# Two-layer hybrid block on one core: gate projections of the mixers spread between other matmuls, and another order of the work at each mixer's entry

## The chip, the cores and the metric

The kernel runs on one core of one Trainium2 chip, as one launch. The metric is the device time of that core in microseconds (us), lower is better. The kernel before was timed three times: 1550.9, 1551.62 and 1552.19 us, median 1551.62 us.

## The reference, cut to what matters

All tensors are float32. A sequence of 256 tokens with 1024 features goes through two layers of a first block and one layer of a second block. Every sublayer is a residual update.

```python
for l in range(2):                                   # first block
    f = swiglu(rms_norm(x, ffn1_pre_g[l]), w_gu, w_down);  x = x + 0.5 * rms_norm(f, ffn1_post_g[l])
    m = hybrid_mixer(rms_norm(x, mix_pre_g[l]), ...);      x = x + rms_norm(m, mix_post_g[l])
    f = swiglu(rms_norm(x, ffn2_pre_g[l]), w_gu, w_down);  x = x + 0.5 * rms_norm(f, ffn2_post_g[l])
# second block: one mixer of other kind (s5, short conv, sparse attention), then one swiglu

def hybrid_mixer(h, ...):
    pa, pb, pc = split(h @ w_in)                     # 768 | 1286 | 512 columns
    gate_a, rec_a = split(pa, 2)
    rec = causal_dwconv(rec_a)
    ya = rg_lru(rec, ...) * gelu(gate_a)             # r, i = sigmoid(...); a = exp(..r); u = sqrt(..tanh..)*(i*rec); scan
    yb = ssd_mixer(pb, ...)                          # conv, silu, decays exp(segsum), (CB * decays) @ (x*dt), norm
    yc = chunk_sgu(pc, ...)                          # u, v = split(gelu(uv)); layer_norm(v); u * (w @ v)
    return concatenate([ya, yb, yc]) @ w_out
```

## The kernel before

**Weights.** All weights come as one stream of chunks of 128 x 1024 float32 (512 KB each), read by the SyncE queue into a ring of six slots (`raw`). Float32 products are made from two parts: ScalarE rounds a chunk to its high part (`split_hi`, line 445, tile `whi`), VectorE or GpSimd subtracts to get the low part (`split_lo`, line 452; `split_lo_pool`, line 461; tile `wlo`), and TensorE makes three matmuls per product (lines 466 to 468: high x high, high x low, low x high). The read of chunk c+6 waits until the low part of chunk c is made; the high part of chunk c+6 waits until TensorE has used chunk c (semaphore `consumed`). Chunks are used in the order of the stream, and `consumed` and `lo_ready` count them.

**Engines.** Each engine has its own instruction list, written by hand; semaphores tie them together. Nothing reorders them. Products land in four banks, `work0` to `work3`; the list `BANKED` says in which order a mixer's results take them, so a result waits (`begin`) until the result four places ahead of it has been taken out. `BY_ACT` and `BY_DVE` say which engine takes it out, and `JOBS` numbers TensorE's finished results.

**A mixer of the first block** (function pairs `mix_pe`, `mix_act`, `mix_dve`, `mix_pool`). TensorE projects `zdt` (z and dt, chunks 0 to 3, the fourth holding only 48 columns in use), `xbc` (chunks 4 to 10), `rec` (11 to 13); then transposes (`xtok0`, `xtok1`), running sums of decays (`csb0` to `csb2`, lines 975 and 976), the recurrence's gates (`lru0` to `lru2`, line 984), `csb3` to `csb5`; then the three gate projections `gate0` to `gate2` (chunks 14 to 16, 24 matmuls of 256 columns each); the six head products `y0` to `y5` (lines 997 to 1001, matmuls of 64 columns); the projections `uv0` and `uv1` (chunks 18 to 21, 24 matmuls of 512 columns each); and the output projection in eight steps. `y3` to `y5` need `weights(1)` of VectorE (line 1196). Before the fourth of the eight output steps stand the small matmuls of `gated` (line 1014), which need the layer norm of `uv` (`vln`, line 1272). ScalarE swaps its function tables (ACT_TABLE_LOAD) between Exp, Sigmoid, Exp and Tanh, Gelu, Sqrt and Gelu. `C_GATE` is 14, `C_PAD` 17 (a chunk of zeros, two columns of which are split), `C_UV` 18.

**Entry into a mixer** (`mix_enter_act`, `mix_enter_dve`), three times: into both mixers of the first block and into the second block's mixer. While TensorE ends the projection before, VectorE updates the first half (t = 0) of x, makes its mean square (`norm_mean`), GpSimd its power (`norm_pow`, line 541, tile `xrstd`), VectorE scales it (`scaled`, line 589, tile `xn`), TensorE transposes it (`turn_xn`, line 647), ScalarE writes its high part (`high`, line 523, tile `xboth`) and VectorE the low part (`low`, line 531). Among these stand the same steps for the second half: `weighted` (line 563), `post_squares` (line 500), `post_mean` (line 545), `update` (line 569). The first matmul of `zdt0` (or of `q0` in the second block) needs the first `low`.

## Time and profile before

| | before |
|---|---|
| median of 3 runs | 1551.62 us |
| the profiled execution, its own time | 1547.13 us |
| its span, first to last instruction | 1545.2 us |
| TensorE (PE) busy | 1479.9 us, 96% |
| VectorE (DVE) busy | 1146.5 us, 74% |
| ScalarE (ACT) busy | 772.0 us, 50% |
| GpSimd (POOL) busy | 140.4 us, 9% |
| mean granted TensorE clock | 0.977 of full speed |

The profile shows one execution. Times inside it count from the start of its span. The first mixer of the first block runs from about 203 to 310 us, the second from about 692 to 801 us, and the second block's mixer begins at about 996 us. The two mixers of the first block repeat each other at a distance of 490.1 us. A wait of TensorE costs time of the kernel wherever TensorE is what sets the end. The granted clock is told as a share of 2.4 GHz: 1.00 is 2.4 GHz and 0.50 is 1.2 GHz.

### The profile page before, as it was taken

How to read it: one execution, taken by the hardware profiler on the slowest of the kernel's cores; microseconds unless marked ns; L12 is line 12 of the kernel's file. 1: busy time of each engine (PE TensorE's matmuls, PEld its weight loads, DVE VectorE, ACT ScalarE, POOL GpSimd, SP SyncE). 2: the span in 40 equal slices, each digit the busy share in tenths (PEclk: the TensorE clock that was granted, in tenths of full speed). 3: DMA queues.
4: the chain of work that ended last, by engine and by line, in shares of the span. 5: the costliest groups of instructions: out<-in, count | busy, mean ns of one | idle time of the engine just before them, and what ended most of it. 6: DMA issues, size and time to landing. Idle time of an engine off the chain costs nothing.

```text
span 1545.2 us, 24303 instructions
## 1 busy us (share of the span) xinstructions
PE 1479.9 (96%) x8495; PEld 1283.3 (83%) x8495; DVE 1146.5 (74%) x1835; ACT 772.0 (50%) x1257; POOL 140.4 (9%) x139
## 2 busy tenths in 40 slices
PE   6999999899999999999899999979998999999999
PEld 5888888788888888879778888777987789888887
DVE  4877776777777777777767777866589967577776
ACT  5344366464444544346645434464588755354432
POOL 0000024100000000005110000101332310000000
PEclk9999999999999999999899999989898999999999
DMA  7665644446655566565344655535522245646652
GB/s 289 193 201 190 192 150 151 132 151 196 201 190 191 208 199 195 188 192 153 109 158 156 204 189 190 166 123 171 192 83 80 72 132 184 190 150 201 194 188 85
DMA packets 71072, 261.74 MB, mean 169 GB/s; under 512 B 8016, under 2 KB 8016, under 8 KB 70736
## 3 DMA queue, kind: packets, MB, share of 16 engines
q1 hardware_dynamic: 69696, 253.79, 50.8%
q10 hardware_dynamic: 1296, 6.85, 1.2%
q8 instruction: 54, 0.88, 0.2%
q14 instruction: 26, 0.21, 0.0%
HBM read 259.56 MB, written 1.05 MB: 169 GB/s over the span
## 4 chain that ended last, share of the span: by engine, by line
PE 87%; DVE 7%; ACT 4%; issue 2%; DMA 1%; POOL 0%; DVEq 0%; ACTq 0%
PE work L728 24%; PE work L729 12%; PE acc L466 8%; PE acc L468 8%; PE acc L467 8%; PE work L466 8%; PE work L467 7%; PE work L468 7%; DVE wlo L452 2%; PE work L1428 1%; PE acc L1457 1%; ACT whi L445 1%; DVE frac L1837 0%; PE work L1429 0%; ACT xboth L523 0%
## 5 line engine op out<-in xcount | busy, mean ns | idle before, releaser
L452 DVE TENSOR_TENSOR wlo<-raw,whi 128x1024 fp32r<-128x1024 f32 x460 | 548.2, 1219 | 206.3 <-ACT whi L445 203.0
L728 PE MATMUL work<-xboth,whi 128*128 128x512 f32 x1600 | 560.7, 393 | 0.0
L445 ACT ACTIVATE whi<-raw 128x1024 fp32r<-128x1024 f32 x480 | 474.9, 1039 | 48.9 <-PE work L468 35.4
L729 PE MATMUL work<-xboth,wlo 128*128 128x256 f32 x1600 | 445.3, 278 | 0.0
L728 PEld LDWEIGHTS work<-xboth,whi 128*128 128x128 f32 x1600 | 299.7, 187 | 68.6
L729 PEld LDWEIGHTS work<-xboth,wlo 128*128 128x128 f32 x1600 | 301.2, 188 | 4.3
L808 ACT ACTIVATE sg<-sg 128x256 f32<-128x256 f32 x100 | 41.8, 418 | 476.1 <-DVE sg L849 476.1
L468 PE MATMUL acc<-whi,hlo 128*128 128x512 f32 x440 | 173.8, 395 | 0.0
L467 PE MATMUL acc<-wlo,hhi 128*128 128x512 f32 x440 | 173.6, 395 | 0.0
L466 PE MATMUL acc<-whi,hhi 128*128 128x512 f32 x440 | 173.5, 394 | 0.0
L466 PE MATMUL work<-xboth,whi 128*128 128x256 f32 x488 | 144.4, 296 | 8.2 <-DVE wlo L452 8.2
L467 PE MATMUL work<-xboth,whi 128*128 128x256 f32 x488 | 141.7, 290 | 0.0
L468 PE MATMUL work<-xboth,wlo 128*128 128x256 f32 x488 | 141.5, 290 | 0.0
L466 PEld LDWEIGHTS work<-xboth,whi 128*128 128x128 f32 x488 | 98.0, 201 | 9.1 <-issue 8.8
L466 PEld LDWEIGHTS acc<-whi,hhi 128*128 128x128 f32 x440 | 82.5, 187 | 19.9
L468 PEld LDWEIGHTS acc<-whi,hlo 128*128 128x128 f32 x440 | 82.5, 187 | 19.9
L467 PEld LDWEIGHTS work<-xboth,whi 128*128 128x128 f32 x488 | 97.9, 201 | 0.1
L468 PEld LDWEIGHTS work<-xboth,wlo 128*128 128x128 f32 x488 | 97.4, 200 | 0.0
L467 PEld LDWEIGHTS acc<-wlo,hhi 128*128 128x128 f32 x440 | 82.5, 187 | 15.7
L466 PE MATMUL work<-whi,xboth 128*128 128x512 f32 (+2 forms) x192 | 79.2, 413 | 13.4 <-DVE wlo L452 8.0
L847 DVE TENSOR_REDUCE sg<-work 128x256 f32<-128x512 f32 x100 | 68.7, 687 | 12.0 <-PE work L729 12.0
L467 PE MATMUL work<-wlo,xboth 128*128 128x512 f32 (+2 forms) x192 | 75.9, 395 | 0.0
(435 smaller groups left out, 2022.0 us busy)
## 6 DMA issues: line engine op xcount, KB each, us to landing
raw<-stream SPq DMA_DIRECT2D x480, 512.0 KB, 3.7
par<-pm ACTq DMA_DIRECT2D x2, 1644.5 KB, 7.3
pfa<-pf_a ACTq DMA_DIRECT2D x3, 516.0 KB, 3.6
pfb<-pf_b ACTq DMA_DIRECT2D x2, 516.0 KB, 8.0
x<-x_in SPq DMA_DIRECT2D x2, 512.0 KB, 5.8
out<-x SPq DMA_DIRECT2D x2, 512.0 KB, 2.6
par<-pm ACTq DMA_DIRECT2D x1, 820.0 KB, 4.3
pre<-pf_a ACTq DMA_DIRECT2D x1, 4.0 KB, 4.0
```

The lines of the kernel that those rows point to most:

```text
L445: nc.scalar.activation(chunk(whi, place, c)[:, cols], chunk(raw, place, c)[:, cols], ACT.Copy).then_inc(hi_ready, 1)
L452: nc.vector.tensor_tensor(chunk(wlo, place, c)[:, cols], chunk(raw, place, c)[:, cols], chunk(whi, place, c)[:, cols].bitcast(F32), ALU.su ...
L466: return [nc.tensor.matmul(o, lhi, rhi, start=start, stop=False), nc.tensor.matmul(o, lhi, rlo, start=False, stop=False), nc.tensor.matmul ...
L467: nc.tensor.matmul(o, lhi, rlo, start=False, stop=False),
L468: nc.tensor.matmul(o, llo, rhi, start=False, stop=stop)]
L728: nc.tensor.matmul(o[:, :], hi[:, k * P:(k + 1) * P], xboth[:, k, :], start=k == 0, stop=False)
L729: m = nc.tensor.matmul(o[:, 0:S], lo[:, k * P:(k + 1) * P], xhi[:, k, :], start=False, stop=k == KD - 1)
L808: nc.scalar.activation(sg[:, j % 2, :], sg[:, j % 2, :], ACT.Silu).then_inc(sg_ready, 1)
L847: nc.vector.tensor_reduce(sg[:, j % 2, :], both_halves(gate), AX.X, ALU.add).then_inc(gsum_ready, 1)
L1428: nc.tensor.matmul(bank2(f"sc{r}", slice(b * S, b * S + nkeys(t))), qT[:, h, t * P:(t + 1) * P], kT[:, 2 * b + h // 4, 0:nkeys(t)], start= ...
L1457: m = nc.tensor.matmul(acc[at:at + 32, 1, k % 2 * S:(k % 2 + 1) * S], left, rotated[:, r % 2, i // 2, i % 2, :], start=i == 0, stop=i == 3)
```

## The change

Three edits.

1. In the mixers of the first block the gate projections no longer stand together. `gate0` comes behind `rec2`, `gate1` behind `csb2`, `gate2` behind `csb5`. ScalarE takes each out with a plain copy, and applies Gelu once to all three (768 columns) behind the Sqrt; VectorE waits for that (`gate_ready`). `uv0` moves ahead of `y0` to `y5`, and its first product now counts the pad chunk as used. The bank order changes with it.
2. `tokens` waits for the low part of each weight chunk when it comes to it, not for the last of them at the start (in all three mixers).
3. At all three entries `scaled` of the first half stands straight behind its mean, and the low part of the fourth chunk (`split_lo [3]`) behind the first two `low`. ScalarE makes the first `high` steps between the two halves of `post_squares`.

```diff
-BANKED = (["zdt0", "zdt1"] + [f"xbc{b}" for b in XBC_ORDER] + ["rec0", "cs", "rec1", "rec2", "xtok0", "xtok1", "csb0", "csb1", "csb2"]
-          + [f"lru{b}" for b in range(AB)] + ["csb3", "csb4", "csb5", "gate0", "gate1", "gate2", "uv0", "uv1", "sgu0", "sgu1"]
+BANKED = (["zdt0", "zdt1"] + [f"xbc{b}" for b in XBC_ORDER] + ["rec0", "cs", "rec1", "rec2", "gate0", "xtok0", "xtok1", "csb0", "csb1", "csb2", "gate1"]
+          + [f"lru{b}" for b in range(AB)] + ["csb3", "csb4", "csb5", "gate2", "uv0", "uv1", "sgu0", "sgu1"]
...
-JOBS += [f"y{h}" for h in range(HEADS)] + ["uv0", "sgu0", "sgu1", "ybt0", "ybt1", "ybt2", "yct0", "yct1"]
+JOBS += ["uv0"] + [f"y{h}" for h in range(HEADS)] + ["sgu0", "sgu1", "ybt0", "ybt1", "ybt2", "yct0", "yct1"]
...
             squares(act, q, 0)
-            post_squares(act, p, 1, end, c)
-            high(act, q, g, range(0, 4))
+            post_squares(act, p, 1, end, c, [0])
+            high(act, q, g, range(0, 2))
+            post_squares(act, p, 1, end, c, [1])
+            high(act, q, g, range(2, 4))
             squares(act, q, 1)
...
             norm_mean(dve, q, 0)
-            split_lo(dve, place, [3])
+            scaled(dve, q, r, 0)
             weighted(dve, p, 1, gp, end)
             post_mean(dve, p, 1, eps[1])
-            scaled(dve, q, r, 0)
             low(dve, q, g, range(0, 2))
+            split_lo(dve, place, [3])
             update(dve, p, 1)
...
-                pe.wait_ge(lo_ready, place.count(c + chunks - 1))
...
                 for k in range(KD):
+                    if k == 0 or ((k + 1) * n - 1) // CH > (k * n - 1) // CH:
+                        pe.wait_ge(lo_ready, place.count(c + ((k + 1) * n - 1) // CH))
...
+                    if padded and k == 0:
+                        recent[0].then_inc(consumed, 1)
...
             channels("rec2", C_REC + 2)
+            channels("gate0", C_GATE)
...
             for h in range(3):
                 sums(h)
+            channels("gate1", C_GATE + 1)
...
-            for b in range(AB):
-                channels(f"gate{b}", C_GATE + b)
+            channels("gate2", C_GATE + 2)
+            begin(pe, BANKED, "uv0")
+            done("uv0", tokens("uv0", 0, C_UV, 2 * CW, padded=True)[-1])
             xdt_ready.wait(pe, T)
...
-                m = nc.tensor.matmul(acc[:, 0, cols], w[:, 0:P], xdt[:, 0, cols], start=True, stop=True)
-                if h == 0:
-                    m.then_inc(consumed, 1)
+                nc.tensor.matmul(acc[:, 0, cols], w[:, 0:P], xdt[:, 0, cols], start=True, stop=True)
...
-            begin(pe, BANKED, "uv0")
-            done("uv0", tokens("uv0", 0, C_UV, 2 * CW)[-1])
             begin(pe, BANKED, "uv1")
...
+            def gated(b):
+                projected(C_GATE + b)
+                emptied(f"gate{b}", nc.scalar.activation(gateT[:, b, :], bank(f"gate{b}", slice(0, S)), ACT.Copy))
+                split_hi(act, place, [C_GATE + b + 6])
+
+            gated(0)
             decays(0)
+            gated(1)
...
             decays(1)
-            for b in range(AB):
-                projected(C_GATE + b)
-                emptied(f"gate{b}", nc.scalar.activation(gateT[:, b, :], bank(f"gate{b}", slice(0, S)), ACT.Gelu_apprx_tanh))
-                split_hi(act, place, [C_GATE + b + 6])
+            gated(2)
             mult2.wait(act, 1)
             mult_ready.inc(nc.scalar.activation(th[:, :, :], th[:, :, :], ACT.Sqrt))
             split_hi(act, place, [C_PAD + 6])
+            evac.wait(act, BY_ACT.index("gate2") + 1)
+            gate_ready.inc(nc.scalar.activation(gateT[:, :, :], gateT[:, :, :], ACT.Gelu_apprx_tanh))
...
-            evac.wait(dve, BY_ACT.index("gate2") + 1)
+            gate_ready.wait(dve, 1)
             ya32.inc(nc.vector.tensor_tensor(rg[:, :, :], rg[:, :, :], gateT[:, :, :], ALU.mult))
```

How the instructions stand. First TensorE in a mixer, from the transposes on. Before, `xtok0` (line 968) is followed by the sums (lines 975 and 976) and the recurrence's gates (line 984):

```order
L968 MATMUL work1<-ident,xbcc 128x128 [waits m_rec_conv,m_xbc_act]
L968 MATMUL work1<-ident,xbcc 128x128 x2
L968 MATMUL work2<-ident,xbcc 128x128 [waits m_vec]
L968 MATMUL work2<-ident,xbcc 128x128 x2
L975 MATMUL work3<-upper,ad 128x256 [waits m_rec_conv]
L976 MATMUL work3<-upper,ad 128x128
L975 MATMUL work0<-upper,ad 128x256 [waits m_rec_conv]
L976 MATMUL work0<-upper,ad 128x128
L975 MATMUL work1<-upper,ad 128x256 [waits m_vec]
L976 MATMUL work1<-upper,ad 128x128
L984 MATMUL work2<-recc,par 128x256 [waits m_rec_conv,m_vec]
```

The same place in the changed kernel, where the lines of code are 975, 982 and 983; it begins at the last matmul of `gate0` and ends at the first three of `gate1`:

```order
L469 MATMUL work1<-xboth,wlo 128x256
L975 MATMUL work2<-ident,xbcc 128x128 [waits m_vec,m_xbc_act]
L975 MATMUL work2<-ident,xbcc 128x128 x2
L975 MATMUL work3<-ident,xbcc 128x128 [waits m_rec_conv]
L975 MATMUL work3<-ident,xbcc 128x128 x2
L982 MATMUL work0<-upper,ad 128x256 [waits m_rec_conv]
L983 MATMUL work0<-upper,ad 128x128
L982 MATMUL work1<-upper,ad 128x256 [waits m_evac]
L983 MATMUL work1<-upper,ad 128x128
L982 MATMUL work2<-upper,ad 128x256 [waits m_vec]
L983 MATMUL work2<-upper,ad 128x128
L467 MATMUL work3<-xboth,whi 128x256 [waits lo_ready,m_vec]
```

A whole gate projection now stands ahead of the transposes and another behind `csb2`; `csb1` waits for ScalarE's copy of `gate0` (`m_evac`) instead of for the convolution.

Then ScalarE in the same stretch, from the end of `rec2`'s split to the first Sigmoids. Before:

```order
L1065 ACTIVATE xbcc<-xbcc 128x256 x3
L445 ACTIVATE whi<-raw 128x1024 x2
L1069 ACT_TABLE_LOAD
L1069 ACTIVATE dm<-dm 128x1152
L1101 ACT_TABLE_LOAD
L1101 ACTIVATE rg<-work,par 128x256
```

and now:

```order
L1070 ACTIVATE xbcc<-xbcc 128x256 x3
L446 ACTIVATE whi<-raw 128x1024 x2
L1106 ACTIVATE gateT<-work 128x256
L446 ACTIVATE whi<-raw 128x1024
L1074 ACT_TABLE_LOAD
L1074 ACTIVATE dm<-dm 128x1152
L1106 ACTIVATE gateT<-work 128x256
L446 ACTIVATE whi<-raw 128x1024
L1114 ACT_TABLE_LOAD
L1114 ACTIVATE rg<-work,par 128x256
```

A copy and a chunk split stand ahead of the decays' Exp and again between it and the Sigmoids; behind the Sqrt one table load and one Gelu of 768 columns come, and the table load ahead of the Gelu of `uv0` is gone.

Last VectorE at the entry. Before:

```order
L545 SCALAR_TENSOR_TENSOR xms<-xss 128x1
L452 TENSOR_TENSOR wlo<-raw,whi 128x48
L563 TENSOR_TENSOR xn<-acc,pfa 128x512 x2
L545 SCALAR_TENSOR_TENSOR pms<-pss,peps 128x1
L589 TENSOR_SCALAR xn<-x,xrstd 128x512 x2
L531 SCALAR_TENSOR_TENSOR xboth<-work,par,xboth 128x128 x4
L569 SCALAR_TENSOR_TENSOR x<-xn,prstd,x 128x512 x2
```

and now:

```order
L546 SCALAR_TENSOR_TENSOR xms<-xss 128x1
L590 TENSOR_SCALAR xn<-x,xrstd 128x512 x2
L564 TENSOR_TENSOR xn<-acc,pfa 128x512 x2
L546 SCALAR_TENSOR_TENSOR pms<-pss,peps 128x1
L532 SCALAR_TENSOR_TENSOR xboth<-work,par,xboth 128x128 x4
L453 TENSOR_TENSOR wlo<-raw,whi 128x48
L570 SCALAR_TENSOR_TENSOR x<-xn,prstd,x 128x512 x2
```

The scaling of the first half moved up past the split, the product and the mean of the second half; the low part of the fourth chunk moved down behind the first low parts of x. In the second block's entry that chunk is a full one of 1024 columns.

## Rows read from the trace of the kernel before

**Rows 1.** Waits of TensorE: total us, times, longest us.

```profile
PE work L466 <- DVE wlo L452: 19.8, 3, 8.2
...
PE acc L997 <- DVE dm L1196: 6.5, 2, 3.2
```

**Rows 2.** Timeline of TensorE, first mixer: start, duration, instruction [idle before, releaser].

```profile
249.38 0.82 PE L968 MATMUL work<-ident,xbcc 128*128 128x128 f32 x6
...
251.73 0.70 PE L975 MATMUL work<-upper,ad 128*128 128x256 f32 x2 [0.88 <-DVE recc L1162]
...
253.58 2.86 PE L984 MATMUL work<-recc,par 128*128 128x256 f32 x12
...
258.88 0.70 PE L975 MATMUL work<-upper,ad 128*128 128x256 f32 x2 [1.79 <-ACT ig L1102]
...
260.34 0.38 PE L466 MATMUL work<-xboth,whi 128*128 128x256 f32 x1
...
269.06 0.33 PE L997 MATMUL acc<-xdt,dm 128*128 128x64 f32 x2
...
274.43 0.43 PE L997 MATMUL acc<-xdt,dm 128*128 128x64 f32 x2 [3.25 <-DVE dm L1196]
...
285.23 0.39 PE L466 MATMUL work<-whi,xboth 128*128 128x512 f32 x1
...
290.67 0.40 PE L466 MATMUL acc<-whi,yahi 128*128 128x512 f32 x1
```

**Rows 3.** Windows: PE, PEld, DVE, ACT, POOL busy (count); granted clock, DMA.

```profile
274.40:278.00 3.60, 3.57 (x19) 3.57 (x19) 3.46 (x5) 0.00 (x0) 0.00 (x0) 0.55 0.37 137
...
768.50:772.00 3.50, 3.50 (x10) 2.73 (x10) 3.27 (x7) 2.50 (x6) 1.35 (x2) 0.50 0.00 0
772.00:776.00 4.00, 4.00 (x17) 3.26 (x16) 3.11 (x4) 0.86 (x1) 2.38 (x3) 0.86 0.46 133
```

**Rows 4.** Timeline of ScalarE, first mixer.

```profile
256.69 1.28 ACT L1101 ACT_TABLE_LOAD   x1
...
259.78 0.50 ACT L1102 ACTIVATE ig<-work,par 128x256 f32<-128x256 f32 x1
...
263.67 0.50 ACT L1107 ACTIVATE th<-rg,psp 128x256 f32<-128x256 f32 x1
...
266.81 1.05 ACT L445 ACTIVATE whi<-raw 128x1024 fp32r<-128x1024 f32 x1
...
272.01 0.84 ACT L1114 ACTIVATE th<-th 128x768 f32<-128x768 f32 x1
```

**Rows 5.** Timeline of VectorE, first mixer.

```profile
271.89 1.22 DVE L452 TENSOR_TENSOR wlo<-raw,whi 128x1024 fp32r<-128x1024 f32 x1
273.02 1.35 DVE L1196 TENSOR_TENSOR dm<-dm,acc 128x1152 f32<-128x1152 f32 x1
```

**Rows 6.** Timeline of VectorE (layer norm's end) and TensorE (`gated`), first mixer.

```profile
296.96 0.42 DVE L1272 TENSOR_TENSOR vx<-vx,par 128x256 f32<-128x256 f32 x1
...
299.07 1.89 PE L1014 MATMUL work<-vx,par 128*128 128x64 f32 x16
```

**Rows 7.** Timelines of GpSimd, ScalarE and VectorE at the first mixer's entry.

```profile
202.06 0.55 POOL L541 TENSOR_TENSOR xrstd<-xms,small 128x1 f32<-128x1 f32 x1 [2.73 <-DVE xms L545]
...
203.27 0.60 ACT L500 ACTIVATE h<-acc 128x512 f32<-128x512 f32 x1 [0.74 <-DVE xn L563]
...
205.13 2.17 ACT L523 ACTIVATE xboth<-work,par 128x128 fp32r<-128x128 f32 x8 [1.18 <-PE work L647]
...
204.12 0.88 DVE L589 TENSOR_SCALAR xn<-x,xrstd 128x512 f32<-128x512 f32 x2
...
205.79 1.13 DVE L531 SCALAR_TENSOR_TENSOR xboth<-work,par,xboth 128x128 fp32r<-128x128 f32 x4 [0.79 <-ACT xboth L523]
```

**Rows 8.** Timelines of GpSimd and VectorE at the second block's entry.

```profile
995.05 1.46 POOL L541 TENSOR_TENSOR xrstd<-xms,small 128x1 f32<-128x1 f32 x1 [3.03 <-DVE xms L545]
...
999.29 1.13 DVE L531 SCALAR_TENSOR_TENSOR xboth<-work,pfa,xboth 128x128 fp32r<-128x128 f32 x4 [0.82 <-ACT xboth L523]
```

More of the change, by code:

```diff
@@ L395, in block_program @@
         ya32 = mixsig("ya32", 1)
+        gate_ready = mixsig("gate", 1)
         dexp = mixsig("dexp", 2)
@@ L490, in halves_of, with post_squares @@
             return slice(h * D // 2, (h + 1) * D // 2)
-        def post_squares(act, p, t, end, c):
-            for h in range(2):
+        def post_squares(act, p, t, end, c, parts=range(2)):
+            for h in parts:
                 if h == 0:
@@ L920, in channels, with tokens @@
                 m[-1].then_inc(consumed, 1)
-            def tokens(name, t, c, n, at=0, first=False):
+            def tokens(name, t, c, n, at=0, first=False, padded=False):
                 chunks = -(-KD * n // CH)
-                pe.wait_ge(lo_ready, place.count(c + chunks - 1))
                 hi, lo = chunk(whi, place, c, chunks), chunk(wlo, place, c, chunks)
@@ L1326, in tokens @@
                 chunks = -(-KD * n // CH)
-                pe.wait_ge(lo_ready, place.count(c + chunks - 1))
                 hi, lo = chunk(whi, place, c, chunks), chunk(wlo, place, c, chunks)
@@ L1330, in tokens @@
                 for k in range(KD):
+                    if k == 0 or ((k + 1) * n - 1) // CH > (k * n - 1) // CH:
+                        pe.wait_ge(lo_ready, place.count(c + ((k + 1) * n - 1) // CH))
                     if first:
```

## The prediction

> **What bounds the kernel now.** I read the share of busy time first: TensorE is busy 96% of the span, so the end moves only where TensorE waits, or where it runs at the lower clock. So I read TensorE's waits next. The longest group, on the low parts of weight chunks, belongs mostly to the second block [rows 1]; its 8.2 us wait there stands behind a chain of VectorE and ScalarE that the change does not touch. The wait of the head products on `weights(1)` is 6.5 us in two times, one in each mixer [rows 1]. The timeline of the first mixer then shows three waits: 0.88 us in front of a sum, 1.79 us in front of another and 3.25 us in front of `y3` [rows 2], 5.92 us together. The windows show what follows the longest one: the granted clock is 0.55 behind it in the first mixer, and 0.50 and then 0.86 in the second [rows 3]. So the wait is paid twice, once as idle time and once as slow matmuls.
>
> **The most that the mixer can give.** From the transposes (249.38) to the output projection (290.67) TensorE takes 41.29 us [rows 2]. Its work at full clock, from the same rows: the three gate projections take 269.06 - 260.34 = 8.72 us, 2.91 each. `uv1` is 24 matmuls of 512 columns from 285.23 to 290.67, 5.44 us, so both uv take 10.88. `y0` to `y2` take 274.43 - 3.25 - 269.06 = 2.12 us, six 4.24. Transposes, six sums and the three `lru` take 260.34 - 249.38 - 0.88 - 1.79 = 8.29 us. The sum is 32.13, which is 9.16 less than 41.29: 5.92 of waits and 3.24 of lower clock (y3 to uv1 took 16.24 us against 13.00 at full clock).
>
> **The new waits in the mixer.** I follow the new order from 249.38.
> `gate0` ends at 252.3. Transposes and three sums: two sums together take 260.34 - 258.88 = 1.46 at most, so these four pieces take about 2.6, and `gate1` starts at about 254.9 and ends at 257.8. ScalarE can take `gate0` out at 252.4 (a copy of 256 columns is priced by the nearest activation, 0.50 or less [rows 4]), which is before the second sum wants the bank, and has split the next chunk (1.05 us) by 253.9, long before the decays' Exp, which waits on VectorE. So the copy and split of `gate0` cost nothing; the cover is ScalarE's idle time in front of that Exp.
> Behind `gate1` it differs. ScalarE copies at 257.9, splits until 259.3, and only then loads the table for the Sigmoids. Before, that load began at 256.69 [rows 4]. So Sigmoid, Exp and Tanh come about 2.6 us later: the last Sigmoid ends at 262.9 instead of 260.28, the last Tanh at 266.8 instead of 264.17 [rows 4]. TensorE meanwhile does `lru` (254.9 + 2.9 = 257.8, to about 260.5; before it took 2.7) and `csb3` to 261.2, then waits for the Sigmoids' banks, some 0.3 us in front of `csb4` and less than 0.1 in front of `csb5` and `gate2`. Together 0.5. `gate2` runs from 262.9 to 265.8.
> `uv0` then wants four chunks one after another. The low parts of the first three are there (VectorE has idle time for them). The fourth stands on VectorE behind three products that need the last Tanh: those ended at 271.89, that is 2.85 us of work, so now 266.8 + 2.9 = 269.7, and with the split of 1.22 [rows 5] the chunk is ready at 270.9. TensorE reaches it after 18 of its 24 matmuls, at 265.8 + 4.1 = 269.9. It waits 1.0 us. This is the one use of edit 2 that matters here: with the old wait TensorE would have stood 5.1 us in front of `uv0`. `y0` starts at 272.3. `weights(1)`, 1.35 us behind that split [rows 5], ends at 272.2, and `y3` wants it at 274.4: the 3.25 us wait is gone with 2 us to spare.
> New waits make 1.5 us. Against that, two sums that started 251.73 and 253.58 took 1.85 us [rows 2], 0.4 more than the pair at 258.88; they waited for banks that VectorE emptied late, and now the `gate0` in front gives it time. So I take 9.16 - 1.5 + 0.4 = 8.1, and for what else of that kind the 8.29 may hold I add 0.4: **8.5 us in the first mixer** (bounds: 6 if each new wait is doubled and that credit is nil; 9.2 if none arises).
> The second mixer's slow stretch is longer. 0.50 instead of 0.55 over about 7.5 us, and 0.86 over 4 us where the first mixer was at full clock [rows 3], is 0.4 + 0.5 us more work at the low rate. **9.3 us in the second mixer.**
>
> **Gelu, Copy and tables.** The Gelu moves behind the Sqrt: a table load of 1.28 and a Gelu of 768 columns, priced as the Sqrt of 768 columns, 0.84 [rows 4]. From mult2 at 269.7: Sqrt, a split, the load and the Gelu end at about 274.5. VectorE's `weights(1)`, product and scans run until 275.1, so the Gelu is hidden by 0.6 us. If it were not, `ya32` and the low part of ya would be late, which the output projection wants only at 281.9; VectorE has that about 2 us earlier. Cost nil.
> The load row is 1.28 us, so it ends at 257.97; the last of the six Sigmoids starts at 259.78, which leaves five activations of 0.36 us each between and no room for more [rows 4]. The Trainium skill, page ScalarE: Activation LUTs, section What ACT_TABLE_LOAD costs, gives about 1283 ns for the load and adds about 1380 ns of drain at each switch. The trace agrees on the load and shows no such drain. By the page, two switches (Sigmoid, Exp) in front of the last Tanh would make it 2.8 us later than in my chain, the wait in `uv0` 3.8 us, and the whole gain some 13.3 instead of 18.9; with the row against it this case is worth 0.01.
>
> **The entries.** In the first mixer GpSimd ends the power at 202.61. Scaling can begin at 202.65; its first half takes 0.44. From the scaled half to the first `high` it took 205.13 - 204.56 = 0.57. So ScalarE begins at 203.66 instead of 205.13, 1.5 us earlier. But now the four activations of the first two steps (0.27 each) come ahead of the second half's square, which took 0.72 to VectorE's mean, and the mean (0.13) stands ahead of the first `low`: 203.66 + 1.09 + 0.72 + 0.13 = 205.6 against 205.79 [rows 7]. So the first matmul comes 0.2 us earlier, not 1.5. The later update of the second half starts where it did: the early mean costs 0.9 on one side and the split of 48 columns is small. Same in the second mixer. In the second block's entry GpSimd took 1.46 us beside a full VectorE split; that split is gone from beside it, so I take 0.55 (bounds 0.55 and 1.46). Then low parts begin at 995.60 + 2.98 = 998.6 instead of 999.29 [rows 8]: 0.7 us (bounds -0.2 and 0.7). The full split of 1.22 us now lies in front of the update of the second half, which is then 0.5 us late, but the matmuls that need it come 3 us after the first. The gain reaches the end, since in ScalarE's list the load of the second block's parameters, and the chain behind it, follow a `high` that waits for TensorE. Entries: 0.2 + 0.2 + 0.7 = **1.1 us**. The later low part also delays the SyncE queue's read six chunks on by about 4.6 us; that chunk is used more than 15 us later, so nothing.
>
> **The sum.** 8.5 + 9.3 + 1.1 = 18.9 us. Against the profiled execution: 1547.1 - 18.9 = 1528.2. That execution lay 4.5 us below the median of the runs, and I carry the difference over: 1551.6 - 18.9 = **1532.7 us**.
>
> **The rivals.**
> A. *As above*, 0.59: 1529 to 1536.
> B. *The clock falls anyway*, 0.15. The y block is 4.2 us of matmuls of 64 columns between a short wait and `uv1`. For it: the windows' 0.55 came right behind matmuls of this kind. Against it: with 0.88 and 1.79 us waits and small matmuls from 249 to 260 the next gate projection still ran at full rate, 2.9 us. It would leave 3.24 us per mixer unpaid: 18.9 - 6.5 = 12.4, 1539.2 us. The Trainium skill, page TensorE: Matmul & The Clock Gate, Part 1, says that the rate follows how busy TensorE has been recently, which would speak for this rival if small matmuls count little.
> C. *The time is given back behind uv*, 0.12. `gated` ran at 299.07, and the layer norm ended at 297.38, 1.7 us before [rows 6]. Now VectorE comes to the layer norm with its list full: it must first make the y sums (behind y5, at about 276.5), ya's low part, two splits and the norm of yb, by my count until about 283, while `uv1` ends at about 281.9. Before, it stood idle there. I count 0.6 to 1.3 us of delay, just inside 1.7. If it takes 3 to 4 us instead, each mixer loses 2 us: 1537 us.
> D. *Slower*, 0.04. One wait decides it: `uv0` stands before its fourth chunk until the Tanh chain is through. It becomes a loss over 0.2% when this wait is 12 us or more a mixer instead of 1.0, i.e. the low part comes after about 281 instead of 270.9; then 2 x 11 - 18.9 = +3.1, 1554.7 us and more. Only a ring of waits among the new bank order could do that; I find none.
> E. *No change*, 0.03: weights' reads become the bound, as TensorE now asks for the chunks of `uv` and the output 9 us sooner; DMA share 0.37 to 0.46 in the windows speaks against [rows 3]. 1551 us.
> F. *A switch of tables costs twice the row*, 0.01: each late step behind two switches, 13.3 us in all, 1538.3 us.
> G. *More*, 0.06: the earlier transposes also keep the clock up at the entries, and no new wait in the mixers: 24 us, 1527.5 us.
>
> **Numbers.** Predicted 1532.7 us. The range goes from G to B, with 2 us beyond B in case part of C comes with it: 1527 to 1541 us. Two executions of this kernel that differ by under 0.2% (3.1 us) can't be told apart. Faster by more than that: A, B, C, F and G, 0.93; within it 0.03; slower 0.04.
>
> **What would show it.** In the changed kernel's trace: no wait of the y products on `weights(1)`; one wait of about 1 us inside `uv0` on a low part and about 0.3 us before the fifth sum; granted clock 1.00 from the transposes to the output projection; that stretch together with `gate0` about 32.6 us long; 45 instead of 47 table loads; at the entries the transposes 1.5 us earlier but the first `zdt0` matmul only 0.2. The prediction is wrong if the clock falls in the y block, if `gated` waits for the layer norm, or if the Sigmoids come more than 3 us later than they did.

## The result and the profile after

The changed kernel takes **1529.71 us** (median of 4 runs, 1526.19 to 1532.01), the kernel before 1551.26 us beside it (4 runs, 1549.57 to 1552.19): the ratio is 0.986 with a 95% interval of 0.9839 to 0.9881. That is 21.55 us less, where 18.9 were forecast; the time forecast was 1532.7 us, between 1527 and 1541. On a second chip the same pair gave 1530.85 against 1549.33 us, ratio 0.9881 (0.9866 to 0.9896), or 18.5 us. The profiled execution after is the longest of its four, 1532.01 us (span 1530.1 us), and lies 15.1 us below the profiled one of before. So the two traces show 6.4 us less than the medians do. Where 5 us of gain go in the profiled pair is told below.

The page of the changed kernel, TensorE and its clock in 40 slices:

```profile
span 1530.1 us, 24313 instructions
...
PE 1474.6 (96%) x8495; PEld 1278.1 (84%) x8495; DVE 1146.3 (75%) x1835; ACT 770.7 (50%) x1257; POOL 140.3 (9%) x139
...
PEclk9999999999999999999999999979998999999999
```

TensorE's waits in the changed kernel (total us, times, longest):

```profile
PE work L467 <- DVE wlo L453: 21.5, 5, 8.2
PE work L467 <- DVE xboth L532: 9.6, 9, 2.0
...
PE work L650 <- DVE xn L590: 2.3, 3, 1.0
PE acc L467 <- DVE xboth L1294: 1.7, 2, 0.9
PE work L982 <- ACT ig L1115: 0.7, 2, 0.3
```

The wait of the head products on `weights(1)`, 6.5 us in two times [rows 1], has no row any more. The waits on low parts went from 3 to 5 times and by 1.7 us: the two new ones are those inside `uv0`. The 1.79 us in front of the fifth sum [rows 2] became 0.33.

TensorE in the first mixer, changed kernel:

```profile
251.39 0.82 PE L975 MATMUL work<-ident,xbcc 128*128 128x128 f32 x6
...
260.63 0.70 PE L982 MATMUL work<-upper,ad 128*128 128x256 f32 x2 [0.33 <-ACT ig L1115]
...
270.15 0.50 PE L467 MATMUL work<-whi,xboth 128*128 128x512 f32 x1 [0.83 <-DVE wlo L453]
...
271.64 0.33 PE L1006 MATMUL acc<-xdt,dm 128*128 128x64 f32 x2
...
281.38 0.39 PE L468 MATMUL acc<-wlo,yahi 128*128 128x512 f32 x1
...
289.55 1.89 PE L1019 MATMUL work<-vx,par 128*128 128x64 f32 x16
```

`gate0` starts at 248.51 and the output projection at 281.15, 32.64 us where the same work took 41.29 [rows 2]. Only waits of 0.33 and 0.83 us are left in it. The windows of the same stretch (PE, PEld, DVE, ACT, POOL busy, granted clock, DMA share, GB/s):

```profile
262.00:266.00 4.00, 4.00 (x32) 3.83 (x31) 2.19 (x5) 3.91 (x9) 0.00 (x0) 1.00 0.63 216
266.00:270.15 4.15, 3.32 (x15) 2.43 (x13) 4.06 (x5) 4.12 (x5) 0.00 (x0) 1.00 0.25 99
270.15:274.20 4.05, 4.05 (x30) 3.79 (x30) 3.95 (x5) 3.27 (x4) 0.00 (x0) 1.00 0.42 130
274.20:278.20 4.00, 4.00 (x26) 3.53 (x25) 3.48 (x7) 1.62 (x4) 0.44 (x2) 1.00 0.01 5
```

The clock is 1.00 (2.4 GHz) in every one, where 0.55 stood before behind the 3.25 us wait [rows 3]. ScalarE and VectorE behind it:

```profile
265.42 0.49 ACT L1120 ACTIVATE th<-rg,psp 128x256 f32<-128x256 f32 x1
...
271.31 1.28 ACT L1127 ACT_TABLE_LOAD   x1
272.61 0.84 ACT L1127 ACTIVATE gateT<-gateT 128x768 f32<-128x768 f32 x1
```

```profile
268.88 1.22 DVE L453 TENSOR_TENSOR wlo<-raw,whi 128x1024 fp32r<-128x1024 f32 x1
270.01 1.35 DVE L1208 TENSOR_TENSOR dm<-dm,acc 128x1152 f32<-128x1152 f32 x1
...
274.44 0.96 DVE L1262 TENSOR_TENSOR rg<-rg,gateT 128x768 f32<-128x768 f32 x1
...
288.19 0.43 DVE L1284 TENSOR_TENSOR vx<-vx,par 128x256 f32<-128x256 f32 x1
```

The Gelu ends at 273.45, 1.0 us before VectorE asks for it. The fourth low part ends at 270.10, where `uv0` resumes. The layer norm ends at 288.62, 0.9 us before `gated` at 289.55; this slack was 1.7 us [rows 6]. The changed kernel has 45 table loads where the kernel before has 47.

TensorE at the first mixer's entry, the turn of the first half and the first product of `zdt0`, first before and then after:

```profile
204.66 1.09 PE L647 MATMUL work<-ident,xn 128*128 128x128 f32 x8 [2.15 <-DVE xn L589]
206.55 0.67 PE L466 MATMUL work<-whi,xboth 128*128 128x390 f32 x1 [0.80 <-DVE xboth L531]
```

```profile
202.67 1.09 PE L650 MATMUL work<-ident,xn 128*128 128x128 f32 x8 [0.68 <-DVE xn L590]
205.78 0.67 PE L467 MATMUL work<-whi,xboth 128*128 128x390 f32 x1 [2.02 <-DVE xboth L532]
```

The turn comes 1.5 us sooner behind the matmul ahead of it (0.68 us of wait for 2.15), and most of that is waited for again in front of the first product.

**Where the gain stands in the two traces.** Starts of the same instructions of TensorE, before and after:

| place | before | after | gained so far |
|---|---|---|---|
| turned second half, mixer 1 | 212.43 | 211.55 | 0.88 |
| behind mixer 1 | 315.87 | 306.49 | 9.38 |
| first `zdt0` matmul, mixer 2 | 695.53 | 685.83 | 9.70 |
| turned second half, mixer 2 | 702.57 | 691.74 | 10.83 |
| behind mixer 2 | 806.83 | 786.63 | 20.20 |
| second block, behind its 8.2 us wait | 1027.91 | 1007.75 | 20.16 |
| end of span | 1545.2 | 1530.1 | 15.1 |

Nearly all that the change touches is through at 20.2 us. The second block's later part has the same code in both, but for the wait per chunk in `kv0` and `kv1`, and the same long waits; it took 5 us longer. The whole of it, first before and then after:

```profile
1027.91:1545.20 517.29, 498.72 (x3203) 438.67 (x3203) 383.67 (x609) 276.05 (x467) 62.19 (x45) 0.97 0.46 149
```

```profile
1007.75:1530.10 522.35, 503.70 (x3203) 442.90 (x3203) 383.75 (x609) 276.07 (x467) 62.13 (x45) 0.95 0.46 147
```

TensorE is idle for 18.6 us in both (517.29 - 498.72 and 522.35 - 503.70). The same 3203 matmuls are what took 5.0 us longer, at a lower mean clock.

The changed kernel's other three runs had mean clocks of 0.982 to 0.984 and spans of 1524.3 to 1528.0 us, the profiled one 0.980. A second trace of the changed kernel, from another chip, has 520.1 us for the part that took 522.35 here, and the other kernels of this study, which do not change that part any further, lie between 517.4 and 521.9. So the profiled pair understates the gain by what the clock did in a part whose work and waits are the same in both. There is one trace of the kernel before; its execution was 4.1 us below the median of its runs, so a part of the difference lies in which executions were profiled. Whether this part runs a little slower behind the change on average is not shown.

**The mixers in all traces.** From the turned second half to the first matmul behind the mixer, us:

| kernel | mixer 1 | mixer 2 |
|---|---|---|
| before | 103.44 | 104.26 |
| changed | 94.94 | 94.89 |
| changed, second trace | 94.96 | 95.00 |
| mixer alone | 94.95 | 94.99 |
| entries alone | 103.45 | 103.56 |
| `uv0` waits for all four chunks | 101.23 | 101.42 |
| head products ahead of `uv0` | 101.49 | 102.46 |
| Gelu at each copy | 96.21 | 96.20 |
| fourth low part early | 93.81 | 93.79 |
| low parts of x ahead of the mean | 95.00 | 94.97 |
| all three, two traces | 93.03, 93.02 | 93.05, 93.00 |
| filled wait | 94.98 | 95.01 |

Where no long wait stands in it, a mixer takes the same time to about 0.1 us in all traces of the same mixer code. These rows therefore say more about each edit in the mixers than the medians can.

### The profile page after: what moved, and what is told of

Its sections match the earlier page's. It is cut to its first block, busy times and chain, and to the rows that moved or that the text cites. A ratio compares the mean times of both kernels' runs of the same rounds, so it can differ in the third digit from the quotient of the medians.

```text
span 1530.1 us, 24313 instructions
## 1 busy us (share of the span) xinstructions
PE 1474.6 (96%) x8495; PEld 1278.1 (84%) x8495; DVE 1146.3 (75%) x1835; ACT 770.7 (50%) x1257; POOL 140.3 (9%) x139
## 4 chain that ended last, share of the span: by engine, by line
PE 86%; DVE 7%; ACT 4%; issue 2%; POOL 1%; DMA 1%; DVEq 0%; ACTq 0%
PE work L731 24%; PE work L732 12%; PE work L467 8%; PE acc L469 7%; PE acc L467 7%; PE work L469 7%; PE acc L468 7%; PE work L468 7%; DVE wlo L453 2%; PE work L1441 1%; ACT whi L446 1%; PE acc L1470 1%; DVE x L570 0%; ACT xboth L524 0%; PE work L1442 0%
## 5 line engine op out<-in xcount | busy, mean ns | idle before, releaser
L538 POOL TENSOR_TENSOR prstd<-pms,small 128x1 f32<-128x1 f32 x12 | 6.6, 548 | 750.9 <-DVE pms L546 750.9
```

The lines of the kernel that those rows point to most:

```text
L538: nc.gpsimd.tensor_tensor(prstd[:, t:t + 1], pms[:, t:t + 1], small[:, 0:1], ALU.pow).then_inc(prstd_ready, 1)
```

## The experiments

The first four ran on one chip, beside 14 runs of the kernel before with a median of 1549.72 us.

**The mixer alone.** The new order and the waits per chunk stay; the entries are as before.

```diff
-            post_squares(act, p, 1, end, c, [0])
-            high(act, q, g, range(0, 2))
-            post_squares(act, p, 1, end, c, [1])
-            high(act, q, g, range(2, 4))
+            post_squares(act, p, 1, end, c)
+            high(act, q, g, range(0, 4))
...
-            scaled(dve, q, r, 0)
+            split_lo(dve, place, [3])
             weighted(dve, p, 1, gp, end)
             post_mean(dve, p, 1, eps[1])
+            scaled(dve, q, r, 0)
             low(dve, q, g, range(0, 2))
-            split_lo(dve, place, [3])
```

> The changed kernel with the order of the entries as before (edits 1 and 2 alone). Theory (the gain lies in the waits of the mixers and the low clock behind them): about 18 us faster than before, with the stretch from the end of rec2 to the output projection 32.6 us long in both mixers against 41.3 before; the first matmul of zdt0 as late after the last matmul of the down projection as before (about 4.4 us). Rival (the entries carry a good part through the clock): under 16 us faster.

Measured: 1532.99 us (1531.51 to 1533.98), ratio 0.9894 (0.9878 to 0.9911), 16.7 us less than before. The waits inside the mixers are 0.33 and 0.83 us as in the changed kernel. By the milestones its mixers gained 8.49 and 9.27 us, as in the changed kernel, and the first `zdt0` matmul stands 4.04 us behind the last matmul ahead, as before (about 4.4 were expected). The mixers carry most of the gain.

**The entries alone.** The kernel before, with the changed entries and the waits per chunk in `tokens`; the gate projections, `uv0`, the Gelu and the table loads as before.

> The kernel before with the entries of the change and the wait for each chunk in turn (edits 2 and 3 alone). Theory: 0.2 us earlier at each of the first two entries and 0.7 at the third, 1 to 2 us in all and within the spread of runs; the transposes start 1.4 us earlier but TensorE waits 2.0 us behind them. Rival (earlier transposes keep the clock up): 4 us or more faster, with the granted clock of the entry's 8 us clearly above 0.8. In the mixers the wait for each chunk alone should change nothing, since y3's wait stands.

Measured: 1546.25 us (10 runs, 1542.57 to 1552.46), ratio 0.9987 (0.9971 to 1.0002), 3.5 us less by the medians, while the interval reaches no change. The two halves add up to 16.7 + 3.5 = 20.2 us, between the 21.55 and 18.5 of the whole on other chips; since the 3.5 may be nothing, the sum shows only that nothing large is missing. The ten runs fall into two groups of five: 1542.57 to 1545.08 us at mean clocks of 0.979 and 0.980, and 1547.42 to 1552.46 at 0.972 to 0.978. None of the 14 runs of before is under 1548.45. The trace is of the first group, and its products behind the waits of 2.02 us at the second and third entry ran at full clock, at the first they did not:

```profile
205.90:211.56 5.66, 5.66 (x24) 5.63 (x25) 4.82 (x12) 1.50 (x5) 1.81 (x2) 0.75 0.25 93
694.45:699.58 5.13, 4.79 (x25) 4.14 (x25) 4.47 (x12) 1.50 (x5) 1.80 (x2) 1.00 0.31 102
995.59:1001.91 6.32, 5.81 (x24) 4.46 (x25) 4.90 (x12) 1.50 (x5) 2.31 (x13) 1.00 0.29 83
```

So the rival (the new entries keep the clock up) is not excluded: it fits this execution, and not the changed kernel's, whose clocks at the same three places were 0.73, 0.71 and 0.76. Its waits show the mixers untouched and the wait of the entries at 2.0:

```profile
PE work L466 <- DVE xboth L531: 10.1, 10, 2.0
PE acc L1000 <- DVE dm L1199: 6.5, 2, 3.2
```

**`uv0` waits for all four chunks.** The changed kernel, with the old form of the wait for `uv0` alone:

```diff
+                if padded:
+                    pe.wait_ge(lo_ready, place.count(c + chunks - 1))
```

> The changed kernel, but uv0 waits at its start for the low part of all four chunks. Theory 1 (a wait is paid once): TensorE stands 5.1 us before uv0 in place of 0.8 inside it, so 3.9 us a mixer, some 8 us slower than the changed kernel. Theory 2 (a wait of this length also drops the clock, as the 3.25 us wait did): the granted clock behind it near 0.5 for some microseconds, about 3 us more a mixer, some 14 us slower than the changed kernel.

Measured: 1542.27 us (1541.78 to 1543.83), ratio 0.9957 (0.994 to 0.9974). Against the ratios of the changed kernel on two chips, 0.9860 and 0.9881, this gives back 12 to 15 us. Its timeline and windows of the first mixer:

```profile
271.86 0.77 PE L467 MATMUL work<-whi,xboth 128*128 128x512 f32 x1 [4.96 <-issue]
```

```profile
266.90:271.80 4.90, 0.00 (x0) 0.00 (x0) 4.05 (x5) 4.87 (x7) 0.00 (x0) 0.79 0.29 107
271.80:275.80 4.00, 3.94 (x9) 3.15 (x10) 3.90 (x5) 3.25 (x4) 0.00 (x0) 0.50 0.44 135
275.80:279.80 4.00, 4.00 (x19) 3.27 (x17) 1.22 (x2) 0.98 (x2) 0.00 (x0) 0.90 0.01 2
279.80:283.60 3.80, 3.80 (x37) 3.80 (x36) 0.00 (x0) 0.00 (x0) 0.00 (x0) 1.00 0.00 0
```

The wait is 4.96 us instead of 0.83 (5.1 were forecast for it), and behind it the clock is 0.50 (1.2 GHz) for 4 us and 0.90 for 4 more: 4 x 0.50 + 4 x 0.10 = 2.4 us. A mixer loses 4.13 + 2.4 = 6.5 us, two lose 13.1; by the milestones they lost 6.3 and 6.5. Idle time and slow matmuls behind it are both needed for the measured loss; idle time alone makes 8.3. The second reason for this kernel's time, that a wait is paid twice, is thereby shown by an edit that adds one.

**The head products ahead of `uv0`.** The changed kernel, with the gates spread, but `y0` to `y5` before `uv0` again:

```diff
-            begin(pe, BANKED, "uv0")
-            done("uv0", tokens("uv0", 0, C_UV, 2 * CW, padded=True)[-1])
             xdt_ready.wait(pe, T)
...
+            begin(pe, BANKED, "uv0")
+            done("uv0", tokens("uv0", 0, C_UV, 2 * CW)[-1])
             begin(pe, BANKED, "uv1")
```

> The changed kernel with y0 to y5 ahead of uv0, gates spread all the same. Theory: y3 waits 4.2 us for weights(1), longer than the 3.25 before, since the gates no longer cover it; by the wait alone 3.2 us a mixer slower than the changed kernel, with the clock's fall 6.5; in all 6.5 to 13 us slower than it. Rival (spreading the gates carries the gain, the place of uv0 is worth little): under 4 us slower than the changed kernel.

Measured: 1543.77 us (1542.56 to 1544.28), ratio 0.9959 (0.9945 to 0.9973), again 12 to 15 us given back. Its timeline and windows:

```profile
272.81 0.69 PE L1004 MATMUL acc<-xdt,dm 128*128 128x64 f32 x2 [4.24 <-DVE dm L1210]
```

```profile
272.90:276.90 4.00, 4.00 (x19) 4.00 (x20) 3.75 (x5) 2.00 (x3) 0.00 (x0) 0.50 0.35 130
276.90:280.90 4.00, 4.00 (x13) 3.13 (x13) 3.88 (x6) 2.00 (x5) 2.00 (x3) 0.62 0.00 0
280.90:284.90 4.00, 4.00 (x19) 3.29 (x18) 2.75 (x5) 0.60 (x1) 1.73 (x2) 1.00 0.59 176
```

The wait on `weights(1)` is back and longer than before, 4.24 instead of 3.25 us, because the gates that filled this time now stand further ahead. Per mixer: 4.24 - 0.83 of waits and 4 x 0.50 + 4 x 0.38 = 3.5 of clock, 6.9 us, 13.9 in two; by the milestones the two lost 6.6 and 7.6. So without the move of `uv0` about 6 of the 20 us are kept, and that with the new entries, which this kernel has too: its mixers are 1.95 and 1.80 us shorter than before, so spreading the gates alone is worth about 3.8 of the 17.9 us that the mixers gained. The two moves are one edit: the gates fill the early waits, and `uv0` takes the place that they left.

The next four ran on another chip, beside 9 runs of the kernel before with a median of 1551.14 us.

**Gelu at each gate's copy.** The changed kernel, with a Gelu of 256 columns in place of each copy and none behind the Sqrt. This adds a table load in front of the Sigmoids' chain.

```diff
-                emptied(f"gate{b}", nc.scalar.activation(gateT[:, b, :], bank(f"gate{b}", slice(0, S)), ACT.Copy))
+                emptied(f"gate{b}", nc.scalar.activation(gateT[:, b, :], bank(f"gate{b}", slice(0, S)), ACT.Gelu_apprx_tanh))
```

> The changed kernel with a Gelu of 256 columns in place of each copy and none behind the Sqrt. ScalarE's list gets more table loads; one of them stands between gate1 and the Sigmoids. By the load's row (1.28 us) the last Tanh, the low part that uv0 waits for and the fifth sum's bank come 1.3 us later: 1.3 us a mixer, 2.6 in all. By 2.66 us for each switch: 2.7 us a mixer or more, over 5 in all. A rival: the second load, ahead of the Sqrt, makes VectorE late too and costs the output projection time.

Measured: 1534.69 us (1529.29 to 1535.58), ratio 0.9884 (0.9866 to 0.9902). Its waits on the Sigmoids and the first of them:

```profile
PE work L981 <- ACT ig L1114: 3.1, 2, 1.6
```

```profile
262.83 0.70 PE L981 MATMUL work<-upper,ad 128*128 128x256 f32 x2 [1.57 <-ACT ig L1114]
...
272.36 0.50 PE L466 MATMUL work<-whi,xboth 128*128 128x512 f32 x1 [0.81 <-DVE wlo L452]
```

The wait before the fifth sum grew from 0.33 to 1.57, by 1.24 us a mixer: the chain is later by one load of 1.28 us and by nothing more. Both mixers took 1.3 us longer. The rival that the load ahead of the Sqrt costs time too is out, since it would come on top of that. In the time the 2.5 us of two mixers can't be told from the changed kernel (ratios 0.9860 and 0.9881); the trace is what settles this.

**The fourth low part ahead of the three products.** The changed kernel with `split_lo(dve, place, [C_UV + 3])` moved up behind that of `C_UV + 2`.

> The changed kernel with the low part of uv0's fourth chunk on VectorE ahead of the three products that wait for the Tanh, not behind them. Theory: the 0.83 us wait inside uv0 goes, weights(1) comes at most as late as now and y3 has slack: 0.8 us a mixer, 1.7 in all. Rival (VectorE's chain to the output projection is as late as TensorE): the wait comes back in front of y3 or of the output projection and nothing is gained.

Measured: 1528.73 us (1525.91 to 1530.53), ratio 0.9856 (0.9841 to 0.9871). Both 0.83 us waits are gone, and nothing came in their place. Each mixer is 1.1 us shorter, more than the 0.8 expected: in the changed kernel the matmul behind this wait starts 1.21 us behind the one ahead and the next one 0.34 us later, where such matmuls else follow each other at 0.23 us, which makes 0.98 + 0.11 = 1.1. The median does not resolve it. The waits on low parts:

```profile
PE work L467 <- DVE wlo L453: 19.7, 3, 8.1
```

**Low parts of x ahead of the mean of p.** At the entries `low(dve, q, g, range(0, 2))` stands before `post_mean(dve, p, 1, eps[1])`.

> The changed kernel with the first two low parts of x on VectorE ahead of the second half's mean at all three entries. Theory (the first matmul waits for the mean that stands ahead of the low part, not for the transposes): first matmul of zdt0 0.9 us earlier, TensorE's wait there 1.1 instead of 2.0 us; 1 to 3 us in all. Rival: the update of the second half comes later and q0 or zdt0 waits at its fifth product.

Measured: 1529.45 us (1528.43 to 1530.15), ratio 0.9861 (0.9846 to 0.9876). The timeline of the first mixer's entry:

```profile
206.39 0.41 PE L467 MATMUL work<-whi,xboth 128*128 128x390 f32 x1 [1.11 <-DVE xboth L532]
...
209.54 0.44 PE L467 MATMUL work<-whi,xboth 128*128 128x390 f32 x1 [0.78 <-DVE xboth L532]
```

The first wait fell from 2.02 to 1.11 us, and a second of 0.78 arose in front of the fifth product: the next x parts are not ready earlier. Most of the 0.9 us goes to this new wait. Of the 1 to 3 us expected the median shows none (ratios 0.9860 and 0.9881 for the changed kernel).

**All three.** The fourth low part early, the low parts before the mean, and the split of the chunk behind `gate1` (`C_GATE + 7`) moved on ScalarE behind the last Sigmoid.

```diff
-                split_hi(act, place, [C_GATE + b + 6])
+                if b != 1:
+                    split_hi(act, place, [C_GATE + b + 6])
...
+            split_hi(act, place, [C_GATE + 7])
```

> The changed kernel with both last steps together, and the high part of one chunk (gate1's place in the ring) moved behind the Sigmoids, so that they start 1.05 us earlier. Theory: the 0.33 us wait in front of the fifth sum goes as well; 1.3 us a mixer from the mixers and 0.9 at each entry, about 5 us faster than the changed kernel. Rival: the clock's dips of one execution and another make more difference than that.

Measured: 1525.65 us (1525.07 to 1526.37), ratio 0.9836 (0.9822 to 0.9849). The waits of 0.33 and 0.83 us are both gone; the longest at the entries is 1.1 us.

The last three ran together on a third chip, beside 9 runs of the kernel before with a median of 1549.33 us: the changed kernel again, the version with all three edits again, and one that fills a wait.

> The changed kernel once more, beside the next two on one chip. 1529 to 1530 us; zdt0's 24 products between 4.3 us (2.4 GHz throughout) and 7.8 us, by where the clock's fall happens to end.

Measured: 1530.85 us (1530.4 to 1531.68), ratio 0.9881 (0.9866 to 0.9896); 1529 to 1530 was expected. The 24 products took 5.91 us at the first entry and 5.13 at the second.

> The kernel with the three further steps again, on one chip with the changed kernel. If they are worth their waits (2.3 us of mixer waits and 2.7 at the entries), 4 to 5 us under it; if the clock gives part of it back, 2 us or less.

Measured: 1524.95 us (1522.85 to 1526.25), ratio 0.9841 (0.9827 to 0.9854). The intervals don't overlap: 5.9 us faster than the changed kernel on the same chip, and the best version of this study. The starts in the two traces place it, 5.97 us of span: 0.91 us ahead of the first entry, in code that is the same, 0.93 in that entry, 1.94 and 2.00 in the two mixers, 0.06 between the mixers and 0.71 between the second and the second block's turned half, less 0.6 behind that. The waits that left the mixers are listed as 0.33 + 0.83 = 1.16 us, and the mixers gained 1.9 to 2.0: a short wait costs somewhat more here than the idle time in its row, since the first matmuls behind it also start further apart.

**A filled wait.** The changed kernel with four more matmuls behind the turn of the first half, whose result nobody reads:

```diff
+            if t == 0:
+                for _ in range(4):
+                    nc.tensor.matmul(acc[:, 0, 0:S], ident[:, :], upper[:, :], start=True, stop=True)
```

> The changed kernel with four matmuls of 256 columns more (identity times a constant, into a bank of acc that nobody needs then) behind the first transposes of each entry, inside TensorE's wait of 2.0 us. Theory (the low clock in zdt0 and q0 comes from the idle time at the entry): granted clock 1.00 through the entry, zdt0 in 4.3 us in both mixers, first matmul not later; 1 to 3 us faster. Rival: the clock falls all the same, or the added matmuls delay the first product, and the time is the same or up to 2 us longer.

Measured: 1529.92 us (1527.83 to 1530.58), ratio 0.9871 (0.9856 to 0.9886). The windows of the first mixer's entry and its timeline:

```profile
204.00:208.00 4.00, 3.71 (x22) 3.18 (x21) 3.31 (x10) 2.85 (x11) 0.55 (x1) 1.00 0.27 107
208.00:212.00 4.00, 3.63 (x20) 2.99 (x19) 3.34 (x8) 1.30 (x4) 1.80 (x2) 1.00 0.47 131
```

```profile
206.73 0.41 PE L467 MATMUL work<-whi,xboth 128*128 128x390 f32 x1 [0.29 <-DVE xboth L532]
...
211.85 1.09 PE L650 MATMUL acc<-ident,xn 128*128 128x128 f32 x8 [0.35 <-DVE xn L590]
```

The same products in the changed kernel's first trace:

```profile
205.78:211.55 5.77, 5.77 (x25) 5.73 (x26) 4.80 (x12) 1.50 (x5) 1.80 (x2) 0.73 0.31 91
```

The clock now stays at 1.00, but the 24 products of `zdt0` take 5.12 us, not the 4.3 expected, with a wait of 0.35 behind them, against 5.77 in the changed kernel: at full rate TensorE comes to the second half before VectorE has scaled it. Against the changed kernel's traces the filling is worth under 1 us an entry, and nothing at an entry where the clock stays up without it (5.13 us at the second entry of its second trace); 1 to 3 us in all were expected, and the 0.9 us measured is within the spread.

## Why the prediction was right

The likeliest case, A, came true. Its steps, in its own order:

- **The new order in the first mixer.** Forecast 32.6 us for the stretch with `gate0`, measured 32.64; 8.5 us gained, measured 8.50 from the turned half to the end of the mixer. (The forecast's own sum gives 41.29 - 8.5 = 32.8 for the stretch, so the closer hit of 32.6 is partly luck.) The wait before the fifth sum was 0.33 us (0.3), the one inside `uv0` 0.83 (1.0). The whole-wait kernel shows that the waits per chunk are worth what was said of them: it stood 4.96 us (5.1).
- **The second mixer.** 9.3 forecast, 104.26 - 94.89 = 9.37 measured. The difference between the mixers is the clock behind the wait of before, as taken (its terms add up to 8.5 + 0.4 + 0.5 = 9.4). But how long the clock stays down is not fixed: with the same wait the second mixer of the kernel with the entries alone took 103.56 us and not 104.26. So 0.7 us of this term belongs to the execution that was profiled.
- **The Gelu.** Hidden, by 1.0 us instead of 0.6.
- **The entries.** 0.2 + 0.2 + 0.7 forecast. The time from the last matmul ahead to the first `zdt0` matmul went from 4.04 to 3.79, and in the second block from 4.86 to 4.09, 0.25 and 0.77; the second mixer's entry gave 0.3. The turn of the first half starts 1.5 us earlier, as forecast, and TensorE then waits 2.02: the chain through the second half's square and mean is the bound, as worked out. The kernel with the low parts ahead of the mean bears that out for the mean: there the wait is 1.11 us.
- **Rival B** (clock falls in the y block) is out: 1.00 in every window. The Trainium skill, page TensorE: Matmul & The Clock Gate, Part 1, ties the rate to how busy TensorE has been recently; the trace agrees in that the rate fell behind the waits of 4.24 and 4.96 us and not behind 0.83, and small matmuls did not lower it here.
- **Rival C** (given back at the layer norm) did not come about, but its slack went from 1.7 to 0.9 us, inside the 0.6 to 1.3 us of delay that were counted.
- **Rivals D and E** fell with the result: the `uv0` wait is 0.83 us, and outside `uv0` the waits on low parts are as long as before (21.5 - 2 x 0.83 = 19.8 us), so later weight reads cost nothing.
- **Rival F** (a table switch costs twice its row) is out by the kernel with the Gelu in place, where one more load cost 1.24 us. The Trainium skill, page ScalarE: Activation LUTs, section What ACT_TABLE_LOAD costs, adds some 1380 ns of drain to the load; no such drain shows.
- **Rival G** (clock kept up at the entries and no new wait in the mixers) didn't come in the profiled execution: the clock was 0.73, 0.71 and 0.76 there, and two waits were left in each mixer. Of its 5 us the larger part lay in the mixers' waits: the kernel with all three steps, which has none of them, is 5.9 us faster than the changed one, 3.9 of it in the mixers. The clock at the entries alone would not have given them, as the filled wait shows. It is partly a matter of the execution: in the second trace of the changed kernel the second entry ran at 1.00.

**What was off** is the last step of the sum, against the medians. By the milestones the changed parts gave 8.50 + 9.37 + 0.25 + 0.32 + 0.77 = 19.2 us, against 18.9. The 20.2 us at the second block hold 1.0 us more, of which 0.5 is at the first transposes, 1.1 in the second mixer's `zdt0` (7.04 to 5.91 us with the same matmuls), and -0.75 in `q0` (6.38 to 7.13). The medians, 21.55 us on one chip and 18.5 on another, lie on both sides of this. Neither was forecast finer than the clock lets two executions agree. Why the medians' gain differs by 3 us between the chips stays open.

## What to carry to other kernels

When an engine waits at several places for chains on others, look for a long block of work that needs none of them, put pieces of it into the early waits, and bring the next such block into the place that they left: the first alone was worth about 3.8 of the 17.9 us here (the second alone was not run). A long operand that arrives in pieces wants a wait per piece, or the move brings the wait with it. In this kernel the waits of 3.25, 4.24 and 4.96 us cost one and a half to twice their length, since the matmuls behind them ran slow; the one of 0.83 us cost 1.1. What the waits of 2.02 us at the entries cost differed from one execution to another. Filling one of them to save the clock gave under 1 us, because VectorE was the next bound there.

## What the runs showed of the hardware that was not expected

The same 24 products of `zdt0` took between 5.01 and 7.10 us over the thirteen traces. The wait in front of them doesn't settle which: behind 0.80 us they took 7.04 us in the second mixer of the kernel before and 5.01 in the kernel with the mixers alone; behind 2.02 us they took 7.10 in the kernel where `uv0` waits for all chunks, and 5.91 and 5.13 in two traces of one and the same kernel, the changed one. The granted clock over them makes the difference:

```profile
695.53:702.57 7.04, 7.04 (x25) 7.00 (x26) 4.68 (x11) 2.15 (x7) 1.79 (x2) 0.58 0.01 5
687.14:692.15 5.01, 4.69 (x24) 4.15 (x24) 4.35 (x11) 2.14 (x7) 1.80 (x2) 1.00 0.00 0
```

Where it stays at 1.00 the products end sooner and TensorE waits about 0.3 us for the second half. So up to 2 us at one place come and go with the execution, and the second block behind its 8.2 us wait took from 517.3 to 522.3 us over the thirteen traces, 520.1 and 522.3 in the two of the changed kernel. When a change is judged from one profiled pair, the milestones on both sides of the changed code say more than the two ends.
